# A decoder trunk on one core: the down projection as seven block products, and another order for the DeltaNet steps

## The reference

```python
def conv_glu_ffn(xn, w_up, conv_w, conv_b, w_down):
    h = causal_dwconv(xn @ w_up, conv_w) + conv_b
    gate, val = jnp.split(h, 2, axis=-1)
    return (jax.nn.silu(gate) * val) @ w_down      # 1024x2816 @ 2816x1024
...
h = x + hybrid_mixer(rms_norm(x, norm1_w), ...)
x = h + conv_glu_ffn(rms_norm(h, norm2_w), w_up, conv_w, conv_b, w_down)
return rms_norm(x, final_norm_w)
```

## Time and profile before

| | us |
|---|---|
| median of 3 runs | 1667.11 |
| lowest and highest | 1665.84, 1668.21 |
| the profiled execution | 1665.57 |
| its span, first to last instruction | 1663.8 |
| mean granted TensorE clock | 0.995 of full speed |
| moved by DMA | 172 MB, 103 GB/s over the span |

### The profile page before, as it was taken

How to read it: one execution, slowest core, us unless ns; L and a number is a source line. 1 busy time by engine, 2 the same in 40 slices (tenths; PEclk the granted TensorE clock), 3 DMA queues, 4 the chain that set the end, 5 groups by cost and what they waited for, 6 DMA issues and landing times.

```text
span 1663.8 us, 20312 instructions
## 1 busy us (share of the span) xinstructions
PE 1624.7 (98%) x8087; PEld 1352.9 (81%) x8087; DVE 786.7 (47%) x1100; ACT 560.4 (34%) x770; POOL 751.5 (45%) x521
## 2 busy tenths in 40 slices
PE   7999999999999999999999998999999999999998
PEld 4888888888887888888888886888888888788886
DVE  5322223353535445364362358555565555545354
ACT  4422221123231253423222235444444444323343
POOL 3335232312222222322424367777777775344583
PEclk9999999999999999999999999999999999999999
DMA  5222431130212133254465212322222322644442
GB/s 167 78 88 76 128 99 39 42 85 21 68 45 75 34 100 88 77 148 129 155 224 202 73 55 64 99 91 76 76 76 90 101 77 101 250 167 152 142 174 102
DMA packets 187051, 172.06 MB, mean 103 GB/s; under 512 B 21476, under 2 KB 155084, under 8 KB 186956
## 3 DMA queue, kind: packets, MB, share of 16 engines
q1 hardware_dynamic: 186736, 170.66, 33.0%
q10 hardware_dynamic: 220, 0.09, 0.0%
HBM read 128.15 MB, written 42.57 MB: 103 GB/s over the span
## 4 chain that ended last, share of the span: by engine, by line
PE 65%; DVE 4%; issue 1%; DMA 0%; SPq 0%; POOL 0%; ACT 0%; DVEq 0%; ACTq 0%
PE acc L555 16%; PE acc L2318 11%; PE acc L2326 7%; PE bank_ab L2318 7%; PE att_ps L2318 5%; PE bank_ab L1401 4%; PE bank_ab L2326 4%; PE att_ps L2326 4%; PE acc L1836 3%; PE bank_ab L1836 1%; PE att_ps L1836 1%; DVE u_t_full L1792 1%; PE att_ps L1476 1%; DVE u_t_low L1796 1%; PE att_ps L1458 1%
## 5 line engine op out<-in xcount | busy, mean ns | idle before, releaser
L966 POOL TENSOR_TENSOR w_low<-w_raw,w_high 128x1024 fp32r<-128x1024 f32 x49 | 117.9, 2406 | 377.7 <-ACT w_high L1048 377.7
L555 PE MATMUL acc<-xh,w_high 128*128 128x512 f32 x832 | 280.7, 414 | 0.6 <-POOL xl L1725 0.6
L555 PE MATMUL acc<-xl,w_high 128*128 128x512 f32 x832 | 262.8, 392 | 0.0
L555 PE MATMUL acc<-xh,w_low 128*128 128x512 f32 x832 | 261.2, 391 | 0.0
L555 PEld LDWEIGHTS acc<-xh,w_low 128*128 128x128 f32 x832 | 156.5, 188 | 34.8
L555 PEld LDWEIGHTS acc<-xl,w_high 128*128 128x128 f32 x832 | 156.5, 188 | 34.2
L555 PEld LDWEIGHTS acc<-xh,w_high 128*128 128x128 f32 x832 | 144.3, 190 | 25.8 <-issue 5.8
L2172 POOL TENSOR_TENSOR f_gl<-f_glu_raw,f_gh 128x1024 fp32r<-128x1024 f32 x39 | 95.1, 2439 | 105.8 <-ACT f_gh L2097 105.7
L2225 DVE TENSOR_TENSOR f_w_low<-u_raw_even,f_w_high 128x512 fp32r<-128x512 f32 x40 | 87.6, 2193 | 102.9 <-ACT f_w_high L2109 102.9
L1139 ACT ACTIVATE sc<-sc,mx 128x128 f32<-128x128 f32 (+1 forms) x96 | 35.4, 440 | 180.4 <-DVE mx L1345 180.4
L2097 ACT ACTIVATE f_gh<-f_glu_raw 128x1024 fp32r<-128x1024 f32 x39 | 41.3, 1060 | 134.5 <-PE att_ps L2326 134.5
(11 more groups left out here) (384 smaller groups left out, 3724.9 us busy)
## 6 DMA issues: line engine op xcount, KB each, us to landing
w_raw<-in_w_in_dram SPq DMA_DIRECT2D x51, 512.0 KB, 4.5
f_glu_raw<-glu_d SPq DMA_DIRECT2D x43, 512.0 KB, 3.6
w_raw<-in_w_up_dram SPq DMA_DIRECT2D x24, 512.0 KB, 5.2
glu_d<-u_free_high SPq DMA_DIRECT2D x22, 512.0 KB, 4.6
u_raw_even<-in_w_down_dram SPq DMA_DIRECT2D x44, 256.0 KB, 3.7
u_raw_even<-in_w_up_dram SPq DMA_DIRECT2D x20, 512.0 KB, 5.0
conv_d<-so SPq DMA_DIRECT2D x16, 512.0 KB, 3.0
gate_d<-qk SPq DMA_DIRECT2D x16, 512.0 KB, 3.1
```

The source lines that it names most:

```text
L555: mm = nc.tensor.matmul(out[:, lo:hi], w, xx[:, lo:hi], start=first and j == 0, stop=last and j == 2)
L966: g.tensor_tensor(wl[:, n % 2], raw[:, n % 2], wh[:, n % 2].bitcast(F32), ALU.subtract).then_inc(s_wlo, 1)
```

## The change

**Down projection.** With glu's k tiles in two halves (0 to 10, 11 to 21), the rows in two (row tiles 0 to 3, 4 to 7) and the columns in two, the 2x2 by 2x2 block product is made of seven products, each of 11 steps (`NP`, `KH`; 77 steps, `NS`). A step's operands are a glu tile of 128x512 and a weight tile of 128x512, or sums of such. VectorE makes the sums of weights (`combine`; three are kept in t1 and t2) and two sums of glu from sums that were made beside the up turns (`glu_sum`, stored to gsum_d), and all low parts of weights (`lows`); GpSimd makes glu's low parts. Products take four banks each, in turn, and each finished product is added to one, two or three results (`add`), four of which are kept as a running sum (`running`, first filled by ScalarE, `keep`). Slots for loads, high and low parts are rings of four. The last three steps are done bank by bank. The loads of h (512 KB each) go with the loads of steps 8 to 15, and the store of the last glu and of its sum comes ahead of the load of step 8.

**Mixer.** While attention units are ready, a DeltaNet step is placed only in slots that have just got an attention item, right behind it; otherwise at odd k as before.

```diff
@@ mixer_schedule
         for k in range(KT):
+            beside = bool(ready)
+            placed = False
             items.append(("mm", n, k))
...
                 items.append(ready.pop(0))
+                placed = True
...
-            if n > 1 + 3 * NH and dn and k % 2 == 1:
+            if n > 1 + 3 * NH and dn and (placed if beside else k % 2 == 1):
@@ ffn, the steps
+    KH = FT // 2
+    NTH = NT // 2
+    TAIL = 3
+    RING = 4
+    NS = NP * KH
+    steps = [(p, kk) for p in range(NP) for kk in range(KH)]
+    glu_summed, w_summed = (3, 5), (0, 1, 2, 6)
...
+    for p, to in enumerate(("00", "u/01", "u/10/11", "01 11", "00", "01", "10")):
+        for i in range(NTH):
+            for name in to.replace(" ", "/").split("/"):
+                adds.append((p, i, name))
@@ sync
+            def load(n):
+                p, kk = steps[n]
+                if n >= RING:
+                    sp.wait_ge(s_low, n - RING + 1)
+                    sp.wait_ge(s_glow, n - RING + 1)
...
-            sp.wait_ge(s_prod, NP * (LAST - 1) + 2)
-            for p in range(2, 5):
-                load(p)
-            store_glu(LAST)
+            sp.wait_ge(s_prod, NP * (LAST - 1) + 3)
+            for n in range(NS):
+                if n == 2 * RING:
+                    store_glu(LAST)
+                    store_sum(LAST)
+                load(n)
...
+                if 2 * RING <= n < 2 * RING + NT:
+                    st = n - 2 * RING
                     sp.dma_start(h[st], halves(h_d[st * P:(st + 1) * P, :])).then_inc(s_h, 16)
@@ scalar
+            def split(n):
+                p, kk = steps[n]
+                loaded(act, n)
+                if n >= RING:
+                    wait_used(act, n - RING)
...
+                for what, to, src in (("w", w_high[:, n % RING, :], w_raw(n)), ("glu", g_high[:, n % RING, :], glu_raw(n))):
...
+                    nc.scalar.activation(to, src, ACT.Copy).then_inc(s_high, 1)
...
+            for n in range(NS):
+                p, kk = steps[n]
+                split(n)
+                if n == RING - 1:
+                    tap0(LAST, 0)
+                if n == RING:
+                    tap0(LAST, 1)
+                if n == RING + 1:
+                    silu(LAST)
...
@@ gpsimd
+            for n in range(NS):
+                p, kk = steps[n]
+                pool.wait_ge(s_high, 2 * n + 2)
+                nc.gpsimd.tensor_tensor(g_low[:, n % RING, :], glu_raw(n), g_high[:, n % RING, :].bitcast(F32),
+                                        ALU.subtract).then_inc(s_glow, 1)
+                if p in (4, 5) and RING + 2 <= kk < RING + 2 + NTH:
...
+                    weighted(*squares[(p - 4) * NTH + kk - RING - 2])
@@ vector
+            def combine(n):
+                p, kk = steps[n]
+                glu, w, more = (slot(n)[:, j, :] for j in range(3))
+                for what, to, x, y, op in {
+                        0: [("w", t1[:, kk, :], more, w, ALU.subtract)],
+                        1: [("w", t2[:, kk, :], w, t1[:, kk, :], ALU.subtract)],
+                        2: [("w", w, t2[:, kk, :], w, ALU.subtract)],
+                        3: [("glu", glu, glu, w, ALU.add)],
+                        5: [("glu", glu, glu, more, ALU.subtract)],
+                        6: [("w", w, w, t2[:, kk, :], ALU.subtract)]}.get(p, []):
+                    loaded(dve, n)
...
+                    nc.vector.tensor_tensor(to, x, y, op).then_inc(s_comb, 1)
+            def lows(n):
+                dve.wait_ge(s_high, 2 * n + 1)
+                nc.vector.tensor_tensor(ups.low_room[n % RING][:], w_raw(n), w_high[:, n % RING, :].bitcast(F32),
+                                        ALU.subtract).then_inc(s_low, 1)
+            def prepare(n):
+                if n + 1 < NS:
+                    combine(n + 1)
+                lows(n)
...
+            combine(0)
+            for n in range(NS):
+                p, kk = steps[n]
+                prepare(n)
+                if n < 3:
+                    mix(LAST, 4 + n)
+                if n == RING:
+                    taps(LAST, 0)
+                if n == RING + 1:
+                    taps(LAST, 1)
+                if n == ahead - 2:
+                    gated(LAST)
+                    glu_sum(LAST)
+                if p and RING <= kk < RING + NTH:
...
+                    add(p - 1, kk - RING)
...
@@ tensor
+            def down(n, i):
+                p, kk = steps[n]
+                rows = slice(i * P, (i + 1) * P)
...
+                for j, (x, w) in enumerate(((a, c), (a, d), (b, c))):
+                    mm = nc.tensor.matmul(row_banks(p)[i], x[:, rows], w, start=kk == 0 and j == 0,
+                                          stop=kk == KH - 1 and j == 2)
...
+            for n in range(NS - TAIL):
+                p, kk = steps[n]
+                ready(n)
+                for i in range(NTH):
+                    if kk == 0:
+                        bank_free(p, i)
+                    mm = down(n, i)
...
```

More of the change, by code:

```diff
@@ L268, in __init__ @@
         self.t_at = base
+        self.xh_at = xh_at
         places = {1: (base, base + 8 * KB), 2: (base + 16 * KB, base + 24 * KB), 4: (base + 32 * KB, base + 40 * KB)}
@@ new lines, in lows, with add @@
+            def lows(n):
[6 more added lines that the diff above has]
+                lows(n)
+            def add(p, i):
+                dve.wait_ge(s_bank, NTH * p + i + 1)
+                if p == 1:
+                    dve.wait_ge(s_one, LAST + i + 1)
+                bank = row_banks(p)[i]
+                mine = [key[2] for key in adds if key[0:2] == (p, i)]
+                for name in mine:
+                    to = result(i, name)
+                    before = [add_no[key] for key in adds[0:add_no[p, i, name] - 1] if key[1:] == (i, name)]
+                    if before:
+                        dve.wait_ge(s_sum, before[-1])
+                    if name != "u" and "u" in mine:
+                        dve.wait_ge(s_sum, add_no[p, i, "u"])
+                        part = running[:, i, :]
+                    else:
+                        part = bank
+                    nc.vector.tensor_tensor(to, to, part, ALU.add).then_inc(s_sum, 1)
@@ L2269, in _ @@
-            dve.wait_ge(s_sq, NT)
-            nc.vector.tensor_scalar(ss0[:], ss0[:], 1.0 / D, EPS, ALU.mult, ALU.add).then_inc(s_ms, 1)
-            dve.wait_ge(s_ms, 1)
-            dve.wait_ge(s_fw, 16)
-            for st in range(NT + 2):
+                if t < LAST:
+                    for n in range(1, 4):
+                        mix(t, n)
+                    glu_sum(t - 1)
+                    mix(t, 4)
+                    mix(t, 5)
+                else:
+                    glu_sum(t - 1)
+                    for n in range(1, 4):
+                        mix(t, n)
@@ L2320, in turn, with ready, bank_free @@
                     mm.then_inc(s_prod, 1)
[L2322 to L2332 removed]
+            def down(n, i):
+                p, kk = steps[n]
+                rows = slice(i * P, (i + 1) * P)
+                a, b = g_high[:, n % RING, :], g_low[:, n % RING, :]
+                c, d = w_high[:, n % RING, :], ups.low_room[n % RING][:]
+                for j, (x, w) in enumerate(((a, c), (a, d), (b, c))):
+                    mm = nc.tensor.matmul(row_banks(p)[i], x[:, rows], w, start=kk == 0 and j == 0,
+                                          stop=kk == KH - 1 and j == 2)
+                return mm
+            def ready(n):
+                pe.wait_ge(s_low, n + 1)
+                pe.wait_ge(s_glow, n + 1)
+            def bank_free(p, i):
+                if p < 2:
+                    pe.wait_ge(s_taken, 2 * (LAST - 1 + p) + 1 + i // 2)
+                else:
+                    last = [n for key, n in add_no.items() if key[0:2] == (p - 2, i)]
+                    pe.wait_ge(s_sum, max(last))
+                    if p == 2:
+                        pe.wait_ge(s_one, LAST + i + 1)
             whole_turn()
```

348 lines of the change are left out of this document (170 added, 178 removed).

## The result

| | before | after |
|---|---|---|
| median, us | 1667.66 (4 runs) | 1642.14 (4 runs) |
| lowest and highest | 1665.84, 1668.82 | 1639.58, 1643.88 |
| the profiled execution | 1665.57 | 1643.88 |
| its span | 1663.8 | 1642.2 |
| mean granted TensorE clock | 0.995 | 0.992 |

The ratio is 0.9845, 95% interval 0.9829 to 0.986: 25.5 us faster. The forecast was 1633 in a range of 1624 to 1648, so sign and range hold and the forecast itself is 9 us too low. The rest of this document is about those 9 us.

A forecast was written before the change was run, and what follows sets the result against it. TensorE, busy 98%, was taken as the bound. From 1665.57 us: -29.9 matmuls, +1.0 additions, +1.7 seam, +0.3 tail, -7.0 and -0.6 DeltaNet gave 1631.1, as a median 1633; range 1624 to 1648.

The forecast's parts named there:

- The matmuls: Down projection: 924 matmuls instead of 1056, 132 fewer at 226.7 ns each, 29.9 us less.
- DeltaNet: Mixer, DeltaNet behind attention: 9.5 us of waits removed, 2.5 added, so -7.0, and -0.6 for fewer switches.
- the places: Mixer: TensorE leaves large products at 138 places instead of 177; 39 fewer give 0 to 4 us, taken 0.6.
- Rival 2: Mixer order gives nothing or costs: +0 to +5 us instead of -7.6, 1641 to 1646 us; chance 0.13.
- The shared stretches: Down projection's preparation: VectorE and GpSimd delay each other, only stretches after release count; stall 0 to 6 us, taken 1.
- rival 1: Down projection: VectorE and GpSimd instructions count with whole durations; 12 to 17 us of stall, 1645 to 1650 us; chance 0.15.
- Tail and up turns: Down projection's last three steps, bank by bank: 0 to 1 us, taken 0.3; added work in up turns: cost 0.
- The seam: Between up and down projection: VectorE, stores and step 8's load stall TensorE, 2 to 5.5 us, taken 4, net +1.7.
- the additions: Down projection: 44 additions of finished products to results, 0.68 us each on VectorE, +1.0 us in the sum.
- a wait of TensorE of 1 to 4 us about 19 us into it: Expected sign early in the down stage: TensorE waits for VectorE's low part, which stands behind a load.
- if the granted clock falls in the stage: Down projection: a fall of TensorE's granted clock there would show the prediction wrong; no size given.
- Rival 3: Down projection: four slots too short for loads; steps stretch at landings over 6.0 us, 1685 us at 8; chance 0.03.

The follow-up runs named there:

- the last version: Changed kernel; second product's tiles refilled in another order, glu stores behind step 12's load, first product's low parts before combinations, last silu, taps, product later: 1631.92 us.
- the late stores: Changed kernel with the last glu and its sum stored behind the load of step 9 instead of ahead of step 8's: 1637.12 us, ratio 0.9825.
- the spread kernel with the low part first: Changed kernel; glu stores behind step 10's load, last turn's second taps, silu and product later, first product's low parts before the next combination: 1633.52 us.
- late stores and the low part first: Changed kernel; glu stores behind step 9's load, and in the first product VectorE's low part ahead of the next step's combination: 1636.37 us, ratio 0.9815.

## Why the prediction was right, and where not

**The matmuls.** 924 of them, at 226.7 ns where nothing waits. 29.9 us, as in the sum.

**DeltaNet.** Predicted -7.6 (-7.0 and -0.6); the stretch from the mixer to the first up matmul is 7.6 us shorter, and alone it gives 0.41% of 1666, 6.8 us. The listed waits from 330 to 900 us were 9.9 us before (4.0 and 3.5 of the earlier trace rows, and 2.4 in four smaller rows) and are 4.2 now, 5.7 less, where the terms said 9.5 removed and 2.5 added. All idle time between the records of TensorE in that stretch fell by the same 5.7 us (13.7 to 8.0), and a large product is followed by a small one 167 times before and 128 times now, 39 places less, as the prediction counted. So the 1.9 us between 5.7 and 7.6 are left for the places, by subtraction. The sum had 7.0 and 0.6: it gained 1.3 us too much from the waits and 1.3 us too little from the places, and that the total came out to a tenth is luck. Rival 2 did not happen.

**The shared stretches.** A step with one combination, one low part and GpSimd's fits. The windows of the late stage show no stall but in the fourth product, where the third product's additions come. There VectorE's and GpSimd's timelines:

```profile
1525.75 1.95 DVE L2354 TENSOR_TENSOR f_h<-f_h,f_running 128x512 f32<-128x512 f32 x2
...
1525.26 1.29 POOL L2241 TENSOR_TENSOR f_gl<-f_raw,f_gh 128x512 fp32r<-128x512 f32 x1 [2.50 <-ACT f_gh L2152]
1529.05 1.30 POOL L2241 TENSOR_TENSOR f_gl<-f_raw,f_gh 128x512 fp32r<-128x512 f32 x1 [2.49 <-ACT f_gh L2152]
```

Two additions, 0.68 us each elsewhere, take 1.95 beside GpSimd's 1.29, 0.6 us more, and GpSimd's starts are 3.79 us apart in these steps instead of 2.72. TensorE waited once for it, 0.8 us:

```profile
PE bank_ab L2468 <- DVE f_w_low L2329: 0.8, 1, 0.8
```

That was all of TensorE's waiting from 1460 us on. Predicted 1, "0 to 6". So four slots cover what rival 1 said they would not. A low part that meets GpSimd's instruction does wait it out (1.77 us at 1419.77 below, against 0.68), but the sum over a step depends on how often the two meet: of the 44 low parts with a raw tile as source from 1448 us on, half took 693 ns or less, and 1787 is the longest (ns min/median/max):

```profile
L2329 DVE TENSOR_TENSOR f_w_low<-f_raw,f_w_high x44: 677/693/1787, 1449.0 to 1622.9; 128x512 fp32r<-128x512 f32 x44
```

**Tail and up turns.** 0.3 predicted and no wait found; 0 and none.

**The seam: the step that failed.** The sum had "A stall of 1 to 4 us", with 0.5 us each for steps 8 to 10, "together 2 to 5.5, and I take 4; net of the 2.3 removed +1.7", above "8". The traces say about 15 gross and about 12.6 net: 13.5 in the two stretches, less 0.9 for the additions. The chain behind the long wait was right, instruction by instruction; its sizes were not, and two things beside it (the waits at other steps, the clock) were not in the sum at all. (Times here are told from the first down matmul, since the stretches before it shifted all of them.) The sign "a wait of TensorE of 1 to 4 us about 19 us into it" came as one of 7.6 us about 22 us into it.
- VectorE came to the taps 7 us late. The prediction had the low part of step 4 done 3.7 us behind the first down matmul (1417.9 against 1414.18); it was done 10.9 us behind it (1421.47 against 1410.59). It counted that low part from the copy that releases it, and not what VectorE has to do ahead of it: six combinations, five low parts and three sums of the last turn, 14 instructions, from the first load's arrival at 1406.87 without a pause from 1408.84 on (14.6 us), three low parts of them 1.1 us longer than 0.68 and three combinations 0.4 to 0.6 longer, at times when GpSimd worked too. From there to the end of the glu product it took 9.6 us (1431.1), of the 9.1 to 11.6 predicted (the terms written there add up to 8.8 to 11.4). So this part of the chain was right and its start wrong. Some of its rows:

```profile
1419.17 0.68 DVE L2325 TENSOR_TENSOR f_t<-f_raw 128x512 f32<-128x512 f32 x1
1419.77 1.77 DVE L2329 TENSOR_TENSOR f_w_low<-f_raw,f_w_high 128x512 fp32r<-128x512 f32 x1
1421.47 2.59 DVE L2261 SCALAR_TENSOR_TENSOR u_conv<-bank_ab,prm,u_conv 128x1023 f32<-128x1023 f32 x2
```

- "1.57 MB at 411 GB/s, 3.8 us": with the 2.0 of the shortest landing the sum had 5.8 us; from the first store's issue to the combination it took 8.2, 2.4 more. The rate of the earlier trace rows belongs to a stream that is running. Here it stood at 2 GB/s before, and the first windows with stores and loads mixed have 180 and 308. The rows nearer to the size were in the text as an upper bound: landings of 5.6 us in this stretch and one of 9.0. In the changed kernel they are, from 1400 to 1460 us (KB, median us to landing):

```profile
f_raw<-in_w_down_dram SPq DMA_DIRECT2D x11, 512.0 KB, 6.3
f_h<-h_d SPq DMA_DIRECT2D x8, 512.0 KB, 7.3
f_raw<-glu_d SPq DMA_DIRECT2D x11, 256.0 KB, 5.0
```

- Steps 0, 1, 5 and 6 and the matmul behind the long wait waited 1.65, 0.54, 0.32, 1.85 and 0.37 us over the pace, none of which the sum had. At step 0 the low part stood behind the combination of step 1, and the two combinations behind weights that landed 6.3 and 7.3 us after their issues (at 1400.52 and 1401.54), soon behind the stores of the turn before (1397.74 and 1398.42):

```profile
1406.87 0.69 DVE L2325 TENSOR_TENSOR f_t<-f_raw 128x512 f32<-128x512 f32 x1 [4.47 <-DMA f_raw<-in_w_down_dram]
1408.84 1.09 DVE L2325 TENSOR_TENSOR f_t<-f_raw 128x512 f32<-128x512 f32 x1 [1.27 <-DMA f_raw<-in_w_down_dram]
```

- The clock. After 7.6 us without a matmul TensorE ran at half of it at first: matmuls 0.43 us apart instead of 0.227, the first 11 distances 4.80 us instead of 2.49, 2.3 us lost. "It is wrong ... if the granted clock falls in the stage" stood among the signs, and it had no price in the sum. The Trainium skill ("TensorE: Matmul & The Clock Gate", "HAM oscillation — how this bites in real kernels") describes such a case, a wait for a DMA behind which the next tile starts cold. The trace agrees (0.51, 0.50, then 0.96).

**Rival 3** said that the ring would be too short for the loads, at landings over 6.0 us. In the steady part they were 3.6 us for the weights (3.7 before) and no step waited for a load. At the seam many were over 6.0, but the long wait isn't the ring's: the weights of step 8 landed 6.1 us after their issue, and the issue was late. With the same ring of four and landings of 7.0 to 8.8 us the last version waited 0.3 to 0.8 us at each of four steps, near what the rival's formula gives (0.3 to 0.9). So it was right on a place and wrong on the stage.

**The median.** The sum gave 1631.1 for the profiled execution, and it took 1643.88, 12.8 more: 10.9 are the seam (12.6 for 1.7), 2.5 the late start, and -0.5 the tail and the additions (12.9 with the rounding). That execution is 1.7 us over the median of its four, where the one before was 1.5 under its own, so the forecast of 1633 is 9.1 us under the median.

## What to carry to other kernels

A transfer whose data comes late blocks every load behind it in its queue: ask not only when it is issued, but what stands behind it, and put it behind as many loads as its reader allows; if its reader is early only because a buffer is shared, change the order in which the buffer is filled. Where several edits crowd into one stretch of a few steps, take landings from the rows of that stretch, not of the steady part, and price a long stop of TensorE with what its clock costs afterwards. When a wait is mended, look for the next narrow place a few steps on: here most mends gave back part of what they won at a later step.

## What the runs showed that was not expected

- The clock's price grew much less than the stop. In the kernels of this document whose clock fell at the seam, the matmuls behind waits of 2.4 to 7.7 us lost 1.6 to 2.8 us to it: 2.3 in the changed kernel, 1.6 with the late stores, 2.1 after a wait of 4.9 in the spread kernel with the low part first, whose window is shown below. With late stores and the low part first two waits of 1.8 and 2.3 us left it at 1.00.

```profile
1440.00:1445.00 5.00, 2.84 (x7) 2.27 (x8) 3.87 (x4) 1.37 (x3) 2.23 (x2) 0.50 1.04 402
```

- In the same stretch the 768 KB of stores and 768 KB of load took 8.2 us, and 7.8 without h beside them; why so much longer than at the rate before and after is left open. Both stores had landed 4.6 us after the first issue (4.0 and 3.9 after their own), the load of step 8 3.5 us later. The stores' own landings and the start of a queue that had stood still are two candidates that no run tells apart.
- In kernels that are the same up to 215 us, an execution can lose 1.6 us to one window of slow clock before 54 us and another not. A comparison of two spans should take that out first; what brings the window on is open.
